# P.V ahead of the turn of P in block 1's mixers, in the two steps of a head pair that hold a P.V call

## The reference

```
def dilated_mixture_attention(q, k, v):
    branches = [dilated_branch(q, k, v, w, d) for (w, d) in DILATED_PATTERNS]
    ...
    num = sum(wts[i][..., None] * branches[i][0] for i in range(len(branches)))
    den = sum(wts[i] * branches[i][2] for i in range(len(branches)))
    return (num / den[..., None]).astype(q.dtype)
...
    mixed = jnp.concatenate([y_pool, y_attn], axis=-1)
    x = x + mixed @ w_out[l]
```

## Time and profile before

| | |
|---|---|
| median of 3 runs | 2549.62 us (2549.46 to 2551.23) |
| the profiled execution | 2551.16 us |
| its span, first to last instruction | 2549.3 us |
| TensorE busy | 2519.0 us (99%), 11989 matmuls |
| weight loads of TensorE | 2063.5 us (81%) |
| VectorE busy | 1329.4 us (52%) |
| ScalarE busy | 566.9 us (22%) |
| GpSimd busy | 1519.6 us (60%) |
| mean granted clock of TensorE | 0.996 |

### The profile page before, as it was taken

One profiled execution on the slowest core, in us unless ns is written; L12 is line 12 of the kernel. 1 busy time (PEld: TensorE's weight loads), 2 busy tenths in 40 slices (PEclk: granted clock), 3 DMA queues, 4 the chain that ended last, 5 costly groups with the idle time before them and its releaser, 6 DMA issues.

```text
span 2549.3 us, 33140 instructions
## 1 busy us (share of the span) xinstructions
PE 2519.0 (99%) x11989; PEld 2063.5 (81%) x11989; DVE 1329.4 (52%) x1568; ACT 566.9 (22%) x1033; POOL 1519.6 (60%) x858
## 2 busy tenths in 40 slices
PE   9999999999999999999999999999999988999998
PEld 7888888778888888888887778888887776888887
DVE  6555527657555315556137666555227656655512
ACT  2110014652111001110015552110013564111000
POOL 5666666436666666666665536666664322666664
PEclk9999999999999999999999999999999999999999
DMA  5223322113322332322332112332233111332232
GB/s 174 96 93 99 99 91 75 59 43 99 99 94 96 99 98 92 99 99 91 99 97 69 54 54 92 98 122 93 96 100 132 56 37 34 99 99 92 97 99 75
DMA packets 66582, 228.76 MB, mean 90 GB/s; under 512 B 8768, under 2 KB 11456, under 8 KB 66112
## 3 DMA queue, kind: packets, MB, share of 16 engines
q1 hardware_dynamic: 64928, 225.67, 27.0%
q10 hardware_dynamic: 1568, 1.88, 0.2%
HBM read 225.43 MB, written 2.10 MB: 89 GB/s over the span
## 4 chain that ended last, share of the span: by engine, by line
PE 96%; DVE 2%; ACT 1%; issue 1%; DMA 0%; DVEq 0%; SPq 0%; ACTq 0%
PE bank L619 28%; PE bank L621 28%; PE bank L620 28%; PE bank L647 2%; PE bank L806 2%; PE bank L791 2%; PE bank L775 1%; PE bank L653 1%; PE bank L776 1%; PE bank L1037 1%; PE bank L1052 1%; PE bank L1029 0%; PE bank L1028 0%; PE bank L945 0%; PE bank L815 0%
## 5 line engine op out<-in xcount | busy, mean ns | idle before, releaser
L583 POOL TENSOR_TENSOR wl<-raw,wh 128x1024 fp32r<-128x1024 f32 x412 | 1036.8, 2516 | 36.3 <-DVE xl L1658 2.0
L578 POOL TENSOR_SCALAR wh<-raw 128x1024 fp32r<-128x1024 f32 x412 | 445.0, 1080 | 974.7 <-PE bank L621 932.9
L619 PE MATMUL bank<-xh,wh 128*128 128x512 f32 x2088 | 815.1, 390 | 0.0
L620 PE MATMUL bank<-xl,wh 128*128 128x512 f32 x2088 | 813.3, 389 | 0.0
L621 PE MATMUL bank<-xh,wl 128*128 128x512 f32 x2088 | 813.1, 389 | 0.0
L621 PEld LDWEIGHTS bank<-xh,wl 128*128 128x128 f32 x2088 | 392.0, 188 | 82.9
L619 PEld LDWEIGHTS bank<-xh,wh 128*128 128x128 f32 x2088 | 392.0, 188 | 80.8
L620 PEld LDWEIGHTS bank<-xl,wh 128*128 128x128 f32 x2088 | 392.1, 188 | 80.2
L619 PE MATMUL bank<-acth,wh 128*128 128x512 f32 (+1 forms) x902 | 346.4, 384 | 0.0
L620 PE MATMUL bank<-actl,wh 128*128 128x512 f32 (+1 forms) x902 | 346.2, 384 | 0.0
L621 PE MATMUL bank<-acth,wl 128*128 128x512 f32 (+1 forms) x902 | 346.2, 384 | 0.0
(11 more groups left out here) (293 smaller groups left out, 2378.5 us busy)
## 6 DMA issues: line engine op xcount, KB each, us to landing
raw<-in_stream SPq DMA_DIRECT2D x412, 512.0 KB, 3.6
x<-in_x SPq DMA_DIRECT2D x8, 256.0 KB, 5.8
w1k<-in_w1k SPq DMA_DIRECT2D x1, 2048.0 KB, 9.1
w1v_low<-in_w1v SPq DMA_DIRECT2D x1, 1024.0 KB, 6.7
w1v_high<-in_w1v SPq DMA_DIRECT2D x1, 1024.0 KB, 8.9
out_dram<-x SPq DMA_DIRECT2D x4, 256.0 KB, 2.4
out_dram<-x SPq DMA_DIRECT2D x1, 768.0 KB, 3.7
invcount<-in_c_invcount ACTq DMA_DIRECT2D x1, 512.0 KB, 5.4
```

The lines of the kernel that those rows point to most:

```text
L578: nc.gpsimd.tensor_scalar(wh[:, h, :, :], src, 1.0, 1.0, ALU.mult, ALU.mult)\
L583: nc.gpsimd.tensor_tensor(wl[:, h, :, :], src, wh[:, h, :, :].bitcast(F32), ALU.subtract).then_inc(split_done, 1)
L619: mm = nc.tensor.matmul(bank, wh[:, slot, k, :], rh, start=start, stop=False)
L620: mm = nc.tensor.matmul(bank, wh[:, slot, k, :], rl, start=False, stop=False)
```

## The change

In TensorE's program of `mixer1`, the two `values` calls of the loop now stand ahead of `turn(g - 2)`. In steps 2 and 6 of a head pair the order becomes scores, fill, P.V, turn. Nothing else is changed, on no engine; the waits go along with the calls.

```diff
                         if g == 2:
                             pe.wait_ge(proj_read, l * U_PROJ + 5)
+                        if s == 2 and j > 0:
+                            values(2 * j - 1)
+                        if s == 6:
+                            values(2 * j)
                         if g >= 2:
                             turn(g - 2)
-                        if s == 2 and j > 0:
-                            values(2 * j - 1)
                         if s == 3 and j > 0:
                             reciprocal_rows(j - 1)
-                        if s == 6:
-                            values(2 * j)
```

## The result

The changed kernel takes 2566.98 us (median of 4 runs, 2566.52 to 2570.28) against 2550.19 us of the kernel before (4 runs too): a ratio of 1.0065 with a 95% interval of 1.0053 to 1.0078. It is slower by 0.65%. The prediction was 2564.7 us, +15.1 us; measured between medians it is +16.8 us, and the profiled execution has a span of 2564.7 us against 2549.3 us, +15.4 us. That this span equals the forecast of the median is a coincidence.

What follows compares the result with a forecast made beforehand. TensorE, busy 2519.0 of 2549.3 us, was taken as the bound. Per layer 2.88 (first pairs) + 4.69 (sixth) = 7.57, for two layers +15.1 on 2549.62: 2564.7 us, range 2561 to 2568.

Steps and rivals of the forecast that it cites:

- TensorE's own gaps: Around each moved P.V call, TensorE's gaps shrink: about 0.05 us won per call, 1.1 us in all.
- The late turn: In step 6 the turn follows P.V, so ScalarE's copy and the key copies behind it come 2.03 us later.
- The collision: At crossings into pairs two to five, second `low_k` meets GpSimd's `wl`; TensorE's scores wait 0.82 us, net 0.77 each.
- The crossing into the sixth pair: With no fill there, the late second `low_k` makes the turn of V start 2.81 us later.
- The sixth pair: Without fill, new waits of 1.13 us (reciprocals' turn) and 0.30 (P.V); with the crossing, 4.69 late per layer.
- A: Rival: the port is free in time, so `wl` does not hold `low_k`; 2552.6 to 2554.6 us; chance 0.13.
- B: Rival: all waits are covered and only TensorE's gaps change; 2548.5 us (-1.1); chance 0.04.
- C: Rival: late work meets GpSimd again at one to three crossings per layer, 2.3 us more; 2569 to 2579; chance 0.08.

Runs made afterwards that it cites:

- the run with the filled pairs: Changed kernel with P.V moved only in the five pairs with a fill, and both `high_k` pieces ahead of ScalarE's copy of P: ratio 0.9993 against the kernel before.
- the key copies first: Changed kernel with both `high_k` pieces of step 6 ahead of the copy of P on ScalarE: ratio 1.0011 against the kernel before.
- The run that takes the meeting away by force: Changed kernel with GpSimd holding `wl` at a pair's end until VectorE's second `low_k` is done: ratio 1.0019 against the kernel before.
- the run with the tokens first: Changed kernel with ScalarE's key copies and, in step 2, its copy of V's tokens ahead of the copy of P: ratio 1.0011 against the kernel before.

## Why the prediction was right, step by step

**TensorE's own gaps.** Right. Fill to P.V took 0.32 (448.48 to 448.80), P.V to the turn 1.88, the turn to the scores 0.41, the three values taken from the earlier trace rows; 0.05 per call was predicted, and the run with the filled pairs shows 0.06. The rule of the Trainium skill that was set beside it (TensorEngine Tiling (Array Packing), Key Properties: a change of mode drains TensorE) counts the changes, which are the same before and after, and would make this term 0. The rows decide otherwise: what stands on either side of a change prices it.

**The late turn.** Right. The copy comes 0.69 behind the turn's start, 0.70 was predicted, and it is late by 451.37 - 448.96 = 2.41. The fill ahead of it was already late by 448.48 - 448.09 = 0.39 from the crossing before, so 2.02 remain; 2.03 was predicted.

**The collision.** Right, and shown by two runs from two sides: with `wl` held back the piece takes 0.69 and the scores do not wait; with the key copies first the piece is not late. The second `low_k` met `wl` 0.47 behind its start (0.48 predicted), ended 0.56 behind it (0.55, from the one row of 400.98) and the scores stood 0.82 late: 457.85, against 456.68 + 0.35 = 457.03. Five pieces per layer take 2.46 to 2.48, as forecast. All ten agree with the rule that was set beside the one row: of the Trainium skill, SBUF — State Buffer, Who interferes with whom, that the later of the two stands still for the whole instruction of the other.

**The crossing into the sixth pair.** Right. The turn of V started at 548.24 instead of 542.89. The mixer started 0.33 earlier in this execution (401.39 against 401.72), so it is late by 5.68; 2.88 from the pairs before and 2.81 here were predicted, 5.69. VectorE's L1803 took 0.69, as GpSimd was free.

**The sixth pair.** The mechanism was right, and the sum was short by 0.3 per layer. The turn of the reciprocals is late by 555.08 - 548.50 + 0.33 = 6.91, which is 1.23 more than at the turn of V; 1.08 was predicted. Of this 0.10 is the semaphore: ScalarE's copy of V's tokens ended at 554.93, and L815 started 0.15 later, not 0.05. The same shows at P.V of step 6: its copy ended at 559.08, and it started at 559.23. The rest, some 0.05, is that the turn of V behind a wait takes 0.06 more (0.66 printed against 0.60). The 0.05 of the sum was an estimate put down without a row. It came out at L775 (`low_k` ended at 457.80, L775 started at 457.85), and not at these two. The half turn of step 46's P was at 563.15 instead of 555.66, late by 7.82, which is 0.91 more; 0.80 was predicted. Of the 0.11 between them, 0.10 is the semaphore at P.V. The end of the mixer is 7.9 late per layer; the sum said 7.57, short by the late starts at two semaphores and by turns that take longer behind a wait.

**The rivals.** A turned on the 0.48 us by which `low_k` comes behind the start of `wl`; they measured 0.47, so `low_k` did not get ahead. The run that takes the meeting away by force gave +5.5, where A's +5.0 stood. B does not hold, though its gain exists (-1.1 us) where nothing is queued behind the late copy. C's price did not come: the first `low_k` stayed ahead of `wh`, by 0.21 (453.17 and 453.38). L1803 was held in two pairs of a layer, for 1.43 and 1.68 instead of 0.69, but it had been held before (1.42, in four pairs), and TensorE has no wait that comes from it.

**The time.** The stretch of the mixers explains 15.7 us of the 16.8 between the medians; the interval of the ratio is 13.5 to 19.9 us, so the rest is within the scatter of the runs. Of the 2.3 us between the forecast of 2564.7 and the median of 2566.98, some 0.6 is the base, which was 2549.62 when the sum was added to it and is 2550.19 with one run more, and 0.6 is the shortfall in the sixth pair.

## What to carry to other kernels

On an engine that executes in order, moving one call ahead of another moves everything that waits for the second one, and then everything queued behind those waiters on their engines. The bill is found by following the delayed instruction to its consumer, and by reading what that consumer's engine has next in its program. Two engines that share a resource may be in step only because both hang on the same event: here the shift of 2 us was covered by itself in the pairs with a fill, and the meeting that it brought about cost 10.2 of the 15.7 us.

## What the runs showed of the hardware that was not expected

An instruction of TensorE that had waited for ScalarE or VectorE started 0.05 to 0.06 behind the end of what it waited for at some places (L775, 457.80 to 457.85; the last turns, 563.09 to 563.15; P.V of the earlier trace rows at 558.78, behind the copy below, 558.73) and 0.14 to 0.15 at others (L815 in the sixth pair, 554.93 to 555.08; P.V of step 6, 559.08 to 559.23; the pooled map in the run with the tokens first, 549.86 to 550.00).

```profile
558.13 0.60 ACT L1289 ACTIVATE sq<-bank 128x512 f32<-128x512 f32 x1 [0.48 <-PE bank L791]
```

Where it is 0.05 or 0.06, the wait that came last is the first or the only one that the program lists for that instruction; where it is 0.14 or 0.15, it is a later one (the second of two at L815, the third of three at P.V and at the pooled map). That this is the cause was not tried.
